# Banks claimed map by map, border work in another order, and a weighted difference put behind the next maximum

## What is computed

```python
def blk(qs):                         # for each block of 128 queries, 4 heads
    a, b = qs
    s1 = einsum('bqhd,bkhd->bhqk', a, k1) * scale      # map 0, d = 48
    s2 = einsum('bqhd,bkhd->bhqk', b, k2) * scale      # map 1
    w = softmax(s1) - lam * softmax(s2)
    return einsum('bhqk,bkhe->bqhe', w, v)             # e = 96
...
y = concatenate([a_out * silu(na_g), b_out * silu(df_g), c_out * silu(cv_g)]) @ w_out
x_new = x + gate * rms(y, g_post)
h  = rms(x, g_pre) * (1.0 + scale) + shift             # hT in the kernel
hc = rms(xc, g_pre) * (1.0 + mod_c[1]) + mod_c[0]      # hcT
```

## Time and profile before

| | us |
|---|---|
| median of 3 runs | 1652.66 |
| lowest, highest | 1650.25, 1654.98 |
| the profiled execution | 1653.44 |
| its span in the trace | 1651.6 |
| PE busy in the span | 1597.0 (97%) |
| DVE busy | 979.8 (59%) |
| ACT busy | 667.6 (40%) |
| mean granted PE clock | 0.991 |

### The profile page before, as it was taken

One profiled execution on the slowest core, in us unless ns is written; L12 is line 12 of the kernel. 1 busy time (PEld: TensorE's weight loads), 2 busy tenths in 40 slices (PEclk: granted clock), 3 DMA queues, 4 the chain that ended last, 5 costly groups with the idle time before them and its releaser, 6 DMA issues.

```text
span 1651.6 us, 22948 instructions
## 1 busy us (share of the span) xinstructions
PE 1597.0 (97%) x8870; PEld 1277.7 (77%) x8870; DVE 979.8 (59%) x1803; ACT 667.6 (40%) x1323; POOL 140.7 (9%) x192
## 2 busy tenths in 40 slices
PE   7999999899999999999999999989999999999898
PEld 6977877687878878878888888865656887788676
DVE  1356454456556655665447787565665467876674
ACT  3365443424323323263313435244554325433653
POOL 4132100000000000002000110000112001000001
PEclk9999999899999999999999999999999999999899
DMA  8221244334654764462223111221003134213100
GB/s 289 81 77 50 103 153 117 80 82 121 190 158 120 155 185 139 148 151 68 92 96 109 56 54 40 92 93 58 1 26 96 48 107 140 58 39 128 52 14 39
DMA packets 171252, 161.36 MB, mean 98 GB/s; under 512 B 40374, under 2 KB 154280, under 8 KB 171112
## 3 DMA queue, kind: packets, MB, share of 16 engines
q1 hardware_dynamic: 151944, 126.97, 26.1%
q10 hardware_dynamic: 16928, 25.27, 4.7%
q0 software_dynamic: 2272, 7.64, 1.4%
HBM read 149.80 MB, written 11.18 MB: 97 GB/s over the span
## 4 chain that ended last, share of the span: by engine, by line
PE 83%; DVE 10%; ACT 4%; issue 2%; DMA 0%; POOL 0%; ACTq 0%; SPq 0%; POOLq 0%; DVEq 0%
PE psum L2596 46%; PE psum L2567 10%; PE psum L2630 7%; PE psum L3139 5%; PE psum L2621 4%; PE psum L3137 2%; PE psum L2775 2%; PE psum L2687 2%; PE psum L2730 2%; DVE arena L1999 1%; PE psum L2669 1%; PE psum L3010 1%; DVE arena L1969 1%; DVE wring_r L2076 1%; DVE arena L2133 1%
## 5 line engine op out<-in xcount | busy, mean ns | idle before, releaser
L2596 PE MATMUL psum<-hT_r,wring_r 128*128 128x512 f32 x1696 | 575.2, 393 | 3.6 <-ACT branch L1745 1.1
L2596 PEld LDWEIGHTS psum<-hT_r,wring_r 128*128 128x128 f32 x1696 | 319.3, 188 | 79.0 <-issue 10.0
L2596 PE MATMUL psum<-arena_r,wring_r 128*128 128x256 f32 (+1 forms) x1360 | 359.1, 333 | 0.7 <-ACT branch L1564 0.5
L1564 ACT ACTIVATE arena<-psum 128x512 f32<-128x512 f32 (+6 forms) x256 | 149.8, 611 | 416.0 <-PE psum L2596 244.2
L2596 PEld LDWEIGHTS psum<-arena_r,wring_r 128*128 128x128 f32 x1360 | 218.3, 190 | 26.2 <-issue 1.8
L2567 PE MATMUL psum<-arena 128*128 128x96 f32 (+9 forms) x1460 | 220.8, 365 | 16.9 <-ACT branch L1745 7.1
L2596 PE MATMUL psum<-arena_r 128*128 128x512 f32 (+1 forms) x720 | 224.5, 350 | 0.0
L2567 PEld LDWEIGHTS psum<-arena 128*128 128x128 f32 (+5 forms) x1460 | 160.8, 189 | 64.7 <-issue 31.9
L2596 PE MATMUL psum<-hT_r,arena_r 128*128 128x512 f32 x448 | 177.8, 397 | 1.8 <-DVE wring_r L2076 1.0
L2630 PE MATMUL psum<-ident,arena 128*128 128x128 f32 (+3 forms) x1104 | 145.9, 277 | 17.4 <-DMA arena<-in_c_ctx 7.4
L2630 PEld LDWEIGHTS psum<-ident,arena 128*128 128x128 f32 (+3 forms) x1104 | 125.2, 142 | 39.6 <-issue 14.6
(11 more groups left out here) (237 smaller groups left out, 1967.8 us busy)
## 6 DMA issues: line engine op xcount, KB each, us to landing
wring<-in_w_in_b SPq DMA_DIRECT2D x54, 512.0 KB, 5.9
arena<-in_w_mod ACTq DMA_DIRECT2D x16, 1536.0 KB, 8.3
wring<-in_w_in SPq DMA_DIRECT2D x16, 1536.0 KB, 6.9
wring<-in_w_out SPq DMA_DIRECT2D x8, 2048.0 KB, 8.4
wring<-in_w_in_a SPq DMA_DIRECT2D x5, 1536.0 KB, 6.6
arena<-x_dram SPq DMA_DIRECT2D x3, 2048.0 KB, 14.6
wring<-in_w_in SPq DMA_DIRECT2D x6, 1024.0 KB, 5.7
arena<-ebias_dram SPq DMA_DIRECT2D x144, 32.0 KB, 1.8
```

The lines of the kernel that those rows point to most:

```text
L1564: return nc.scalar.activation(out, in_, ACT.Copy, scale=scale)
L2596: ins_ = nc.tensor.matmul(b[0:hi.shape[2], 0:width], w[:, k], v[:, k], start=k + p == 0, stop=(k, p) == (KT - 1, 2))
```

## The change

- `gate B 4` stands ahead of `qm B` in the order, no longer behind it.
- A new step `xr` on DVE, ahead of `hcT 0`, does `final_rows(TT - 2)`, which `xf` did behind it.
- In C1 `nv` stands ahead of `nq`; in C0 it stays.
- `hcT 1` stands right behind the last dT of C0, no longer behind the last doT. The list `split_starts`, which numbers the places of split weights, takes its third boundary from the last doT; the boundary's value is the same.
- `oN` stands ahead of C1's `yv` and `yc` steps of its iteration.
- DVE's part of dS: the maximum and negative of map 0 come first, then `diff_combine` of the item before, then those of map 1.
- PE's part of dS: it claims map 0's banks and makes both its products, then claims and makes map 1's. Before it claimed all and went from map to map. For context items, which have one product for each map, only the claims move.
- `split_features` for gate B 0 and nkc's first group, and nk's own loop: the products with x_hi come first and wait for ACT's x_hi alone; the wait for DVE's x_lo stands ahead of the last.

```diff
-    for i in range(4):
+    for i in range(5):
         add("a", "gate", "B", i)
     add("av", "qm", "B")
-    add("a", "gate", "B", 4)
     add("a" * 8, "mS", "B")
...
+    add("", "xr")
     add("vvvv", "hcT", 0)
     add("", "xf")
...
-        add(lat_ctx * 3, "nq", l)
+        if l == 0:
+            add(lat_ctx * 3, "nq", l)
         add("aaaavv", "nv", l)
+        if l:
+            add(lat_ctx * 3, "nq", l)
...
             add("a", "dT", l, t, h)
+            if n > len(items) and l == 0:
+                add("vvvv", "hcT", 1)
...
         beside(n)
+        if n >= 2 and h == 0 and i:
+            add("", "oN", l, tiles[i - 1])
         if n >= 2 and l:
             for half, q in YO_SPLITS.get(n, ()):
                 add("", "yv", half, q)
...
         if n >= 2:
-            if h == 0 and i:
-                add("", "oN", l, tiles[i - 1])
...
     add("v", "doT", l, last)
-    if l == 0:
-        add("vvvv", "hcT", 1)
-    else:
+    if l:
         add("", "yx", l, before)
...
-        split_starts = [("wout", "A"), ("wout", "B"), ("hcT", 1)]
+        split_starts = [("wout", "A"), ("wout", "B"), ("doT", 0, TT - 1)]
...
+                elif kind == "xr":
+                    final_rows(TT - 2)
                 elif kind == "xf":
-                    final_rows(TT - 2)
                     norm_scale("C0", TT - 2)
...
-                    if (t, h) != diff_items(l)[0]:
-                        diff_combine(n - 1)
                     for i in range(2):
                         full(dve, key, i)
                         chained(nc.vector.reduce_max(d_max[:, p, i:i + 1], halves(t, i), AX_XY if t < TT else AX_X))
                         scaled(d_neg[:, p, i:i + 1], d_max[:, p, i:i + 1], -diff_scale).then_inc(diff_negmax, 1)
+                        if i == 0 and (t, h) != diff_items(l)[0]:
+                            diff_combine(n - 1)
...
+                    passes = ((hi, x_hi), (hi, x_lo), (lo, x_hi))
                     if key[0] == "nkc" and i == 0 and k % 2 == 0:
-                        evacuated(pe, ("hcT", key[1]), k // 2)
-                    if new and i == 0:
-                        evacuated(pe, new, k)
-                    for p, (w, v) in enumerate(((hi, x_hi), (hi, x_lo), (lo, x_hi))):
+                        turned, last_k, b_ = ("hcT", key[1]), k + 1, k // 2
+                    else:
+                        turned, last_k, b_ = new if i == 0 else None, k, k
+                    if turned:
+                        pe.wait_ge(hi_ready, hi_at(turned, last_k))
+                        passes = ((hi, x_hi), (lo, x_hi), (hi, x_lo))
+                    for p, (w, v) in enumerate(passes):
+                        if turned and p == 2:
+                            evacuated(pe, turned, b_)
...
                     for k in range(KT):
+                        pe.wait_ge(hi_ready, hi_at(("hT", f"C{l}"), k))
+                        for g, (hi, lo) in enumerate(parts):
+                            nc.tensor.matmul(banks[g], hi[:, k], hT_hi[:, k], start=k == 0, stop=False)
+                        for g, (hi, lo) in enumerate(parts):
+                            nc.tensor.matmul(banks[g], lo[:, k], hT_hi[:, k], start=False, stop=False)
                         evacuated(pe, ("hT", f"C{l}"), k)
                         for g, (hi, lo) in enumerate(parts):
-                            for p, (w, v) in enumerate(((hi, hT_hi), (hi, hT_lo2), (lo, hT_hi))):
-                                ins_ = nc.tensor.matmul(banks[g], w[:, k], v[:, k], start=k + p == 0, stop=(k, p) == (KT - 1, 2))
+                            ins_ = nc.tensor.matmul(banks[g], hi[:, k], hT_lo2[:, k], start=False, stop=k == KT - 1)
...
-                    for half in range(2):
-                        claim(pe, key, half)
                     tt = t % TT
...
-                        for part in range(2):
-                            cut = slice(part * KEYS // 2, (part + 1) * KEYS // 2)
-                            for half in range(2):
+                        for half in range(2):
+                            claim(pe, key, half)
+                            for part in range(2):
+                                cut = slice(part * KEYS // 2, (part + 1) * KEYS // 2)
                                 ins_ = product(psum[:, 2 * half + part, 0:KEYS // 2], [(q[half], dkT[rows[half], h, cut])])
-                                if part:
-                                    done(ins_)
+                            done(ins_)
```

## The result

The changed kernel takes 1657.9 us (median of 18 runs, 1655.25 to 1661.43), the kernel before in the same session 1653.74 (18 runs). The ratio is 1.0026, with a 95% interval of 1.0018 to 1.0034: 4.2 us slower, which so many runs can tell from nothing, and which still lies within the 0.3% that the prediction called no change. The profiled execution of the changed kernel took 1655.25 us, the shortest of the 18; its span is 1653.4, so it is only 1.8 longer than before's span.

The account below looks back on a forecast made before the run. TensorE, busy 97% of the span, bounds the kernel. Terms -10.0, -3.95, -0.7, +12.8, +3.45 give +1.6, the clock +1.0: 1656.0 us for the profiled run, forecast median 1655; own range 1648 to 1661, full range 1645 to 1666.

Parts of the forecast that it names:

- xr: One row operation moved ahead of hcT 0 on DVE, which was idle there: 0.
- hi ahead of lo: At both nk and gate B 0, x_hi matmuls no longer wait for DVE's x_lo: -1.8, -1.65 and about -0.5, sum -3.95 us.
- Gate B 4: Start of B: moved ahead of qm B, it lets the w_in_b load land earlier, removing idle and half clock: -10.0 us.
- Rival 4: Start of B: weights late for another reason, ACT still stands there, the 10 us remain: 1665 us, chance 0.05.
- The weighted difference: Differential attention: standing between the two maxima, it delays everything behind the second by 1.38 us; summed over places, +12.8 us.
- hcT 1: C0's tail: DVE's 16 operations run ahead of the evacuation that frees bank 7 for yo(0,3): +3.45 us, clock +2.6 besides.
- nv ahead of nq: Layer 1: stalls of 0.97 and 0.48 go, a wait of 0.75 for nvF's last copy comes: -0.7 us.
- Banks map by map: dS: grouping the eight score matmuls by array half costs nothing against alternating them: 0.
- Rival 3: dS: the scores run one half after the other, +35 us over 32 latent items: 1690 us, chance 0.06.
- The clock: Half-clock stretches: +2.6 us behind the idle before yo(0,3), -1.6 at 1560.9, the two others stay: net +1.0.
- Rival 1: The border's gain stands and half clock at 1110 and 1547 goes too, none coming at yo(0,3): 1646 us, chance 0.24.
- Rival 2: Layer 0's tail: paired stalls at doT and yo bring half clock, +8.8 us: about 1664 us, chance 0.20.

Follow-up runs that it names:

- n_F: The changed kernel with the weighted difference back ahead of both maxima, all else kept: 1641.35 us, 0.9921 of the kernel before.
- n_D: The changed kernel with hcT 1 back behind the last doT: 1656.16 us, 1.0012 of the kernel before.
- o_A: The kernel before with one edit, gate B 4 ahead of qm B: 1641.06 us, 0.9921 of the kernel before.
- after_look: The changed kernel unaltered, run once more for a second trace: 1659.41 us.
- n_FD: The changed kernel with both the weighted difference and hcT 1 back in their old places: 1635.16 us, 0.9887 of the kernel before.
- n_FD_pool: n_FD with GpSimd's mask addition for C1's unit pair (1, 0..2) made behind VectorE's scaling, not beside it: 1634.27 us, 0.9886 of the kernel before.

## Why the prediction was right, and where it was off

It gave 1655 and a range of 1645 to 1666; the time is 1657.9, and the sign of the sum was right. Most of it is right term by term. The terms of xr and of hi ahead of lo are read from the stages alone; no kernel undid them.

- **Gate B 4**: -10.0 forecast, -10.3 in the stage of the changed kernel and -10.6 alone. The wait that took the old one's place was put at 0.85 and was 0.83 to 1.48 in the traces: the copy takes 0.68, and in most kernels DVE comes to it late, because the lo part of the late load is made first. Rival 4 (the 10 us remain) is out.
- **The weighted difference**: +12.8 forecast, 16.5 by undoing it. The two don't compare as they stand: the 12.8 has 1.3 in it that oN's move gives back, which n_F keeps, so the forecast for n_F's edit is 14.1, and its stages give 14.7. C0's steady part was put at 3.5 + 1.7 + 1.4 = 6.6 and is 6.7 to 6.8; C1's at 4.5 and is 4.4. The step from "1.38 late, 0.5 spare" to 0.9 at doT held: the gap reads 0.70, and from dS to doT the start is 0.9 later. What failed is the row for the context items, -0.2, which is +1.0 in one trace and +4.4 in the other: I had counted waits for the exponentials and not those of dT for the difference itself (two gaps of 0.7), and not that half clock can come with them. The same step failed in C1's first items, though the size came out. I had the waits for the exponentials at 1530 and 1547 growing; the changed kernel has no such wait there, and dT waits 1.10 twice in their place. n_F is at 43.4, the changed kernel at 46.0, so 2.6 with oN's move in both, where 3.2 had been counted.

```profile
1528.09 0.87 PE L2640 MATMUL psum<-ident,arena 128*128 128x128 f32 x6 [1.10 <-DVE arena L2018]
...
1545.46 0.87 PE L2640 MATMUL psum<-ident,arena 128*128 128x128 f32 x6 [1.10 <-DVE arena L2018]
```

- **hcT 1**: +3.45 and 2.6 for the clock, 6.05 together. By the stage it is 5.5, of which at most half of the 3.4 us at 0.50 is clock, so some 3.8 and 1.7. The chain (16 operations, evacuation, bank 7) is there as told. The clock term was mis-sized by 0.9. Its reason was a misreading: the idle just ahead of the stretches at 1110.3, 1547.2 and 1560.9 is 1.29, 1.74 and 2.27, so none has the size of 3.5. The gain of 0.45 at nkc is too high as well: before's row at 1267.56 has 0.20 of idle. And I hadn't foreseen that in the sum of medians most of this cost disappears (n_D).
- **hi ahead of lo**: nk gave 1.74 and 1.81, where 1.8 and 1.65 stood. Gate B 0 gave nothing for its 0.5: 0.93 became 0.88. DVE's first x_lo of hT B starts at 264.37 and ends near 265.05, with PE's next matmul at 265.21; the weight split that the profile names as releaser had ended at 264.46. hT B holds all eight banks, so gate B 0 can't have a bank before DVE has read one of them. I had looked at the data that it waits for and not at its claim. This is read from the code and these times; no kernel tested it.
- **nv ahead of nq**: -0.7 forecast, 0 found. The new wait is 0.63 for 0.75. But the move takes nq's and nv's steps on SP and POOL with it, the bias loads come earlier, and GpSimd's addition meets VectorE's scaling: 0.99 at nT. I had followed the step on PE, ACT and DVE alone.
- **Banks map by map**: 0 forecast; 1.57 for 1.56 us on PE. Rival 3 is out, and with it the reading of program order by which the second map's matmuls would have to wait for the first's to finish: one behind the other, the eight would take some 2.7 us (an estimate from yo's eight of 512 columns in 3.70). I had put no gain on the other side; the kernels show one between nothing and 1 us in the context items.
- **The clock**: the net of +1.0 for the profiled run was made of +2.6 and -1.6. In the trace 1547, which was to stay, went as well as 1560.9. That gave back more than was counted: o_A against before puts 6.8 us at 0.50 at 2.0 us in C1's first items, so all 10.2 are some 3.0 (an estimate) where 1.6 stood. Rival 1 had that, and would have had 1646; it fell because hcT 1's stretch came and the context items kept theirs. Rival 2 put the half clock into C0's steady part, where neither trace has any behind 0.7 and 0.5.

Stage by stage the forecast for the profiled execution, 1656.0, is close to its 1655.25: start of B -10.0 for -10.3, C0's steady part +6.6 for +6.8, C0's tail +6.05 for +5.5, C1's steady part +4.5 for +4.4, and nothing is off by more than 1.3. The error of 2.9 us in the median comes from elsewhere. I took the median 0.8 below the profiled execution, as it was in the kernel before, and it lies 2.65 above. No term of the sum had this; that the executions of the changed kernel differ by stretches of half clock is what after_look shows for one of them. In C1's first items it is luck that 1.9 was near: taking the clock's 3.0 out, the stage lost some 2.1, but not by the waits that the 1.9 was made of.

## What to carry to other kernels

An operation that seems to gain by going first must be weighed against all that stands behind it in its engine's order; here 1.4 us of VectorE, moved out of a wait into a busy chain, cost 15 to 16 us over 40 items, and two moves undone with the rest kept made a kernel 1.1% faster than before. The best line of a mixed change was an order in which a buffer's last reader came earlier, so that the next load started earlier: look in the trace for an engine whose idle time ends with a DMA, and ask who freed the slot. Half of a stretch at half clock is its cost only where PE would not have waited behind it anyway. When a step moves, follow it on GpSimd and SyncE as well, and look at the claim of its bank, not only at its data.

## What the runs showed of the hardware

Two engines slow each other: a VectorE scaling of 128x512 that takes 0.44 us alone (0.88 for two) took 1.8 to 2.0 for two when a GpSimd tensor addition began beside them, so some 1.0 us more; the addition took 1.28 to 1.59 us in such meetings, where 1.28 is usual. Ordering the addition behind the scaling brought the scaling back to 0.88 and the addition to 1.27 to 1.30.

The half clock doesn't follow from a stall's size alone. In C1's first items nearly the same stalls of 1.0 to 1.1 us were followed by 13.7 us at 0.50 in one kernel and by none in two traces of another, and two executions of one kernel differ by a whole stretch of 6.8 us at 0.50 in the context items. A local gain of 5.5 us came out as 1.7 in the median (n_D), and as 6.2 in a kernel with less idle time around it.

What a stretch at half clock costs depends on what PE waits for behind it. In C1's first items n_FD ran 3.4 us at 0.50 and n_FD_pool none, and both took 43.4 us: the scores that took longer at 0.50 used up the 1.14 us in which PE otherwise stands for an exponential. Windows over the same work, first n_FD and then n_FD_pool (columns as in the earlier trace rows), and PE's next row in n_FD_pool:

```profile
1533.60:1536.90 3.30, 3.30 (x17) 3.30 (x17) 3.23 (x6) 1.88 (x5) 0.00 (x0) 0.50 1.02 411
1533.80:1537.10 3.30, 2.16 (x19) 1.95 (x19) 3.23 (x6) 1.88 (x5) 0.00 (x0) 1.00 1.01 405
```

```profile
1536.89 2.46 PE L2575 MATMUL psum<-arena 48*128 48x384 f32 x8 [1.14 <-ACT arena L1911]
```

The Trainium skill, "TensorE: Matmul & The Clock Gate", section "What's actually happening", says that the clock has these two levels and that the activity of the array sets which is granted. The rows at 1.00 and 0.50 agree with the two levels; what brings a fall, no run here isolates.
